# First attention: sums' inverses through memory, one value product for two query tiles, bias rows loaded four tiles ahead

## The chip, the cores and the metric

The kernel runs on one core of one Trainium2 chip. The metric is device time in microseconds (us) of one execution; the runs are of the same program, and their median is the figure.

## What is computed

The program is a transformer block with forgetting attention, then a two-layer block (RWKV, differential attention, memory attention), 1024 tokens of width 1024, all in float32. The change lies in the forgetting attention of the first block, eight heads of 64 channels:

```python
def forgetting_attention(q, k, v, log_f):
    c = jnp.cumsum(log_f, axis=1).transpose(0, 2, 1)
    ...
    scores = jnp.einsum('bqhd,bkhd->bhqk', q_i, k) * scale
    scores = scores + c_i[:, :, :, None] - c[:, :, None, :]
    scores = jnp.where(causal, scores, -jnp.inf)
    probs = jax.nn.softmax(scores, axis=-1)
    return jnp.einsum('bhqk,bkhd->bqhd', probs, v)
```

## The kernel before

`mixer` yields `att.steps_across(...)`: four pairs of heads, eight tiles of 128 queries each, 32 tiles in all. Tile iq (0 to 7) of a pair sees (iq + 1) x 128 keys. For a tile, in the names of the table `ORDER`:

- C, `Scores`: TensorE multiplies queries by keys (L1817), both heads side by side on the two halves of the array's rows, into banks 0 and 1 (head 0) and 2 and 3 (head 1). It waits for `biased` of the tile before, for those banks.
- M0 and M1, `Biased`: VectorE adds the bias of one head and takes the row maximum (L1841), then negates it (L1844). It writes one of four rows of `sc`, so it waits until the tile two before is wholly transposed. The bias comes from GpSimd, which masks a broadcast row (L2160) that SP loads once a pair (L2141).
- X0 and X1, `Exponentials`: ScalarE, with the row's sum (L1858).
- N, `Normalise`: VectorE's two reciprocals of the sums (L1867, L1869), and a wait for the second.
- V0, V1, V2, `Values`: TensorE transposes up to four 128 x 128 blocks a head (L1895) into bank 4 (head 0) and bank 5 (head 1); ScalarE copies bank 4 (L1925), VectorE bank 5 (L1934), to `pt`, four buffers of 512; TensorE multiplies by the values (L1913), the heads side by side on the halves of the array's columns. V0 transposes the first four blocks; V1 transposes the rest and multiplies the first four; V2, only for tiles 4 to 7, multiplies the rest. For tiles 0 to 3, V1 only multiplies. The product comes out transposed: channels on partitions, queries along the row.
- D, R, A, `Diagonals`, `Spread`, `ScaleAcross`: the inverses stand one to a partition but are needed along the row. ScalarE makes two diagonal matrices of them (L2101), TensorE multiplies by ones (L2114), ScalarE copies the result (L2121), and VectorE multiplies the output by it (L2129).

`ORDER` sets each engine's queue: in iteration t the engine takes each step for tile t plus the number behind the colon. Engines meet only at semaphores. TensorE does, in iteration t, V0 of t, R of t - 1, C of t + 2, V1 and V2 of t. VectorE does N and the V0 copy of t, M0 of t + 2, the V1 copy of t, M1 of t + 2, A of t - 1. Behind the last tile a `Join` stops every engine until all are done. Inside the stage two weight tiles are split by the way (L881 on GpSimd, L895 on ScalarE, L900 on VectorE).

```python
    ORDER = {
        "pe": "V0:0 R:-1 C:2 V1:0 V2:0",
        "dve": "N:0 V0:0 M0:2 V1:0 M1:2 A:-1",
        "act": "X0:1 V0:0 R:-1 D:0 V1:0 X1:1",
        "pool": "C:2",
        "sp": "C:2",
    }
```

## Time and profile before

| | us |
|---|---|
| median of three runs (lowest, highest) | 2948.1 (2946.89, 2953.39) |
| the profiled execution, its own time | 2947.62 |
| its span in the trace | 2946.4 |
| the stage: first scores of L1817 to the last L2129 | 223.6 to 365.1 |
| TensorE busy over the whole span | 2732.0 |
| mean granted TensorE clock, share of full | 0.966 |

The page gives busy time by engine, the span in slices, the chain that ended last, and the costliest groups of instructions. A float32 matmul stands as two instructions (two passes), a transpose as one. The duration of a TensorE instruction in the trace includes its way through the array, so instructions in a row overlap; what a group costs the engine is the distance from its start to the next group's start. A bracket behind a row tells the idle time ahead of it and what ended it.

### The profile page before, as it was taken

The page shows a single profiled execution, that of the slowest core. Times are in us where ns is not written, and L with a number is a line of the kernel's source. Part 1 is how long each engine was busy: PE and PEld are TensorE (multiplying, and loading weights), DVE is VectorE, ACT ScalarE, POOL GpSimd, SP SyncE. Part 2 cuts the span into 40 slices and gives each one's busy share as a digit, 9 for nine tenths or more (in the row PEclk, how much of TensorE's full clock was granted, in tenths as well). Part 3 has the DMA queues.
Part 4 walks back from the last instruction along what each step waited for, and adds up shares of the span by engine and source line. Part 5 has one row for each costly group of instructions (what it writes and reads, how often), then busy time and mean ns, then how long its engine had stood idle before and what let it go on. Part 6 is the DMA issues. An engine that isn't in the chain of part 4 may idle for free.

```text
span 2946.4 us, 49632 instructions
## 1 busy us (share of the span) xinstructions
PE 2732.0 (93%) x20750; PEld 2197.7 (75%) x20750; DVE 1372.9 (47%) x2528; ACT 926.5 (31%) x1854; POOL 634.7 (22%) x631
## 2 busy tenths in 40 slices
PE   8999989999999999999999988888879999989879
PEld 6785667888888888777888856787857878766557
DVE  4336674333333334443455306777554333366652
ACT  3226743211111111243121123444453122244441
POOL 1003253111111111325111102222113202134341
PEclk9999999999999999999999996999989999999889
DMA  3121031121111111112111210010023201122232
GB/s 122 47 72 37 22 130 58 36 72 51 43 50 51 43 50 43 51 57 86 58 32 41 75 45 2 4 32 4 4 93 114 79 15 53 39 53 55 61 81 114
DMA packets 161438, 160.33 MB, mean 54 GB/s; under 512 B 9152, under 2 KB 134714, under 8 KB 159682
## 3 DMA queue, kind: packets, MB, share of 16 engines
q1 hardware_dynamic: 161218, 157.17, 17.6%
q8 instruction: 166, 2.72, 0.4%
q14 instruction: 54, 0.44, 0.0%
HBM read 135.07 MB, written 22.08 MB: 53 GB/s over the span
## 4 chain that ended last, share of the span: by engine, by line
PE 81%; DVE 7%; ACT 4%; POOL 3%; issue 3%; DMA 3%; SPq 0%; DVEq 0%; ACTq 0%; POOLq 0%
PE ps L935 14%; PE ps L937 13%; PE ps L936 13%; PE ps L2520 7%; PE ps L990 5%; PE ps L992 5%; PE ps L991 5%; PE ps L1817 3%; PE ps L1563 2%; PE ps L1996 2%; PE ps L1565 2%; PE ps L1564 2%; DMA sb<-in_w_ffn_gate 1%; PE ps L1895 1%; DVE r L900 1%
## 5 line engine op out<-in xcount | busy, mean ns | idle before, releaser
L935 PE MATMUL ps<-r,r 128*128 128x512 f32 (+1 forms) x1760 | 698.9, 397 | 2.7 <-DVE r L900 1.9
L937 PE MATMUL ps<-r,r 128*128 128x512 f32 (+1 forms) x1760 | 684.8, 389 | 0.0
L936 PE MATMUL ps<-r,r 128*128 128x512 f32 (+1 forms) x1760 | 684.1, 389 | 0.0
L881 POOL TENSOR_TENSOR sb<-sb 128x1024 f32<-128x1024 f32 x117 | 232.2, 1994 | 1221.8 <-DMA sb<-in_w_ffn_up 482.4
L935 PEld LDWEIGHTS ps<-r,r 128*128 128x128 f32 x1760 | 332.3, 189 | 94.1 <-issue 24.2
L937 PEld LDWEIGHTS ps<-r,r 128*128 128x128 f32 x1760 | 331.9, 189 | 69.2
L936 PEld LDWEIGHTS ps<-r,r 128*128 128x128 f32 x1760 | 332.7, 189 | 66.0 <-issue 1.7
L900 DVE TENSOR_TENSOR r<-sb,r 128x1024 fp32r<-128x1024 f32 x182 | 236.6, 1317 | 306.3 <-ACT r L895 306.2
L990 PE MATMUL ps<-r,r 128*128 128x512 f32 (+1 forms) x768 | 301.9, 393 | 38.4 <-DVE r L900 16.0
L2520 PE MATMUL ps<-sb 64*64 64x64 f16 (+2 forms) x8832 | 271.0, 216 | 32.0 <-issue 11.0
L2520 PEld LDWEIGHTS ps<-sb 64*64 64x64 f32 (+1 forms) x8832 | 254.4, 126 | 56.7 <-issue 37.0
L992 PE MATMUL ps<-r,r 128*128 128x512 f32 (+1 forms) x768 | 294.1, 383 | 0.0
L991 PE MATMUL ps<-r,r 128*128 128x512 f32 (+1 forms) x768 | 293.7, 382 | 0.0
L895 ACT CAST r<-sb 128x1024 fp32r<-128x1024 f32 x182 | 186.5, 1045 | 253.1 <-POOL sb L881 203.7
L990 PEld LDWEIGHTS ps<-r,r 128*128 128x128 f32 x768 | 147.9, 193 | 74.4 <-issue 26.7
L992 PEld LDWEIGHTS ps<-r,r 128*128 128x128 f32 x768 | 147.9, 193 | 27.6
L991 PEld LDWEIGHTS ps<-r,r 128*128 128x128 f32 x768 | 148.3, 193 | 26.6 <-issue 1.2
L1563 PE MATMUL ps<-r,r 128*128 128x512 f32 x352 | 139.4, 396 | 7.6 <-DVE sb L1576 6.9
L1528 ACT CAST r<-sb 128x512 fp32r<-128x512 f32 x44 | 27.3, 621 | 378.4 <-DVE sb L1536 378.4
L1565 PE MATMUL ps<-r,r 128*128 128x512 f32 x352 | 137.6, 391 | 0.0
L1564 PE MATMUL ps<-r,r 128*128 128x512 f32 x352 | 137.6, 391 | 0.0
L1841 DVE CUSTOM_DVE_ANT_0 sb<-ps,sb 128x128 f32<-128x128 f32 (+7 forms) x160 | 120.8, 755 | 33.7 <-PE ps L1895 18.1
(266 smaller groups left out, 3421.1 us busy)
## 6 DMA issues: line engine op xcount, KB each, us to landing
sb<-in_a_w_in SPq DMA_DIRECT2D x29, 512.0 KB, 3.9
sb<-in_w_out SPq DMA_DIRECT2D x24, 512.0 KB, 5.2
sb<-in_w_ffn_gate SPq DMA_DIRECT2D x22, 512.0 KB, 4.5
sb<-in_w_ffn_up SPq DMA_DIRECT2D x22, 512.0 KB, 3.9
sb<-in_w_ffn_down SPq DMA_DIRECT2D x22, 512.0 KB, 3.5
sb<-in_w_in SPq DMA_DIRECT2D x17, 512.0 KB, 4.2
xs<-sb SPq DMA_DIRECT2D x4, 2048.0 KB, 7.1
gates<-sb SPq DMA_DIRECT2D x32, 256.0 KB, 2.1
```

Source lines behind the costliest of these rows:

```text
L881: pool.tensor_tensor(w.raw, w.raw, w.gain.unsqueeze(2).broadcast_to((P, w.nk, w.n)), ALU.mult).then_inc(*s.w_gain.up(w.id))
L900: dve.tensor_tensor(w.lo, w.raw, w.hi.bitcast(F32), ALU.subtract).then_inc(*s.w_lo.up(w.id))
L935: pe.matmul(self.out, w.hi[:, q, self.cols], hi, start=(q == 0), stop=False)
L936: pe.matmul(self.out, w.hi[:, q, self.cols], lo, start=False, stop=False)
L937: ins = pe.matmul(self.out, w.lo[:, q, self.cols], hi, start=False, stop=(q == w.nk - 1))
L990: pe.matmul(self.out, hi, w.hi[:, j, :], start=(q == 0), stop=False)
L991: pe.matmul(self.out, hi, w.lo[:, j, :], start=False, stop=False)
L992: ins = pe.matmul(self.out, lo, w.hi[:, j, :], start=False, stop=(q == nk - 1))
L1563: pe.matmul(self.out, hi, w.hi[:, 0, span_of(self.c)], start=(q == 0), stop=False)
L1564: pe.matmul(self.out, hi, w.lo[:, 0, span_of(self.c)], start=False, stop=False)
L1565: ins = pe.matmul(self.out, lo, w.hi[:, 0, span_of(self.c)], start=False, stop=(q == 1))
L2520: ins = pe.matmul(self.bank(b + p // n, n, w)[o, p % n, :], lhs[o, p], rhs[o, p], start=(j == 0 and not onto and not (keep and p)), stop=( ...
```

## The change

- `Values` is split. T0 and T1 (`TurnedAcross`) transpose blocks 0 to 3 and 4 to 7 of a tile; the copies go to `pt[h]`, one buffer a head of 8 key blocks x 2 query tiles x 128, in which an even and the next odd tile lie side by side. W (`ValuesAcross`), on odd tiles alone, multiplies both tiles at once: 256 columns for the key blocks that both see, 128 for the one that only the odd tile sees (tile 1 has three products of 128). It waits for every copy of both tiles. The copies wait until W of the tiles before has read the buffer.
- D and R on ScalarE and TensorE are gone, and with them one copy on ScalarE. N (`Inverted`) writes the reciprocals of a pair of tiles side by side and doesn't wait for itself. R (`SpreadRows`), on odd tiles, is now three DMAs on SP: the inverses to memory (2 KB in pieces of 8 bytes), and from there one row of 256 broadcast to 64 partitions for each head.
- A multiplies 256 columns at once, on odd tiles alone, two iterations behind.
- TensorE's order is T0, T1, C, W. SP takes the load of a pair's bias rows four tiles ahead in its order and, behind it, R. The load still waits until the masks of the last tile of the pair before are made.

```diff
@@ -146,7 +146,7 @@
         self.x = self.at(self.X, ST, D)
         self.ring = tuple(self.RING + j * self.SLOT for j in range(self.SLOTS))
         self.scratch = {n: nc.dram_tensor(n, shape, F32).ap() for n, shape in (
-            ("negc", [ATT_H, S]), ("xs", [P, ST, D]), ("gates", [P, KT, S]), ("memkv", [2, P, 1024]),
+            ("negc", [ATT_H, S]), ("xs", [P, ST, D]), ("gates", [P, KT, S]), ("memkv", [2, P, 1024]), ("inverse", [2 * ST, 2, P, 2]),
             ("pairs", [BT * ST // 2, P, 2]))}
         self.n_ids, self.n_banks, self.product_banks = 0, 0, 4
         self.free = {}
@@ -1653,7 +1653,7 @@
         if diff:
             self.turned = k.at(pt, ST, 2, P)
         else:
-            self.pt, self.diag = [k.at(at, HALF) for at in pt], k.at(on, 2, 2, P)
+            self.pt, self.spread = [k.at(at, ST, 2, P) for at in pt], [k.at(at, 2 * P) for at in on]
         self.heads = 1 if diff else 2
         self.per_pair = sum(self.of_tile(iq) for iq in range(ST))
 
@@ -1695,24 +1695,24 @@
         return out
 
     ORDER = {
-        "pe": "V0:0 R:-1 C:2 V1:0 V2:0",
-        "dve": "N:0 V0:0 M0:2 V1:0 M1:2 A:-1",
-        "act": "X0:1 V0:0 R:-1 D:0 V1:0 X1:1",
+        "pe": "T0:0 T1:0 C:2 W:0",
+        "dve": "N:0 T0:0 M0:2 T1:0 M1:2 A:-2",
+        "act": "X0:1 T0:0 T1:0 X1:1",
         "pool": "C:2",
-        "sp": "C:2",
+        "sp": "C:4 R:0",
     }
 
     def steps_across(self, fill=lambda t, place: []):
 
         last = self.n * ST - 1
-        kinds = {"C": (Scores,), "M0": (Biased, (0,)), "M1": (Biased, (1,)), "X0": (Exponentials, (0,)), "X1": (Exponentials, (1,)), "N": (Normalise,),
-                 "V0": (Values, 0), "V1": (Values, 1), "V2": (Values, 2), "D": (Diagonals,), "R": (Spread,), "A": (ScaleAcross,)}
+        kinds = {"C": (Scores,), "M0": (Biased, (0,)), "M1": (Biased, (1,)), "X0": (Exponentials, (0,)), "X1": (Exponentials, (1,)), "N": (Inverted,),
+                 "T0": (TurnedAcross, 0), "T1": (TurnedAcross, 1), "W": (ValuesAcross,), "R": (SpreadRows,), "A": (ScaleAcross,)}
         made, out = {}, []
-        for t in range(-3, last + 3):
+        for t in range(-4, last + 3):
             for engine, names in self.ORDER.items():
                 for name, ahead in (word.split(":") for word in names.split()):
                     at = t + int(ahead)
-                    if not 0 <= at <= last or name == "V2" and len(self.groups(*divmod(at, ST))) < 3:
+                    if not 0 <= at <= last or name == "T1" and at % ST < 4 or name in "WRA" and at % 2 == 0:
                         continue
                     if (name, at) not in made:
                         kind, *more = kinds[name]
@@ -1735,10 +1735,6 @@
 
     def of_tile(self, iq):
         return self.heads * ((self.nkeys(iq) // P + 3) // 4)
-
-    def pt_before(self, g):
-
-        return g - len(self.pt)
 
     def last_group(self, i, iq, h):
         return [g for g, h2, _, _ in self.groups(i, iq) if h2 == (0 if self.diff else h)][-1]
@@ -1877,63 +1873,6 @@
                                      ALU.mult, ALU.add).then_inc(*s.combined.up((of.id, i, iq, 0)))
 
 
-class Values(AttentionStep):
...
@@ -2089,44 +2028,118 @@
         pool.tensor_tensor(self.y, self.y, self.gate, ALU.mult).then_inc(*s.pair_gated.up((of.id, n)))
 
 
-class Diagonals(AttentionStep):
...
+class TurnedAcross(AttentionStep):
+
+    def __init__(self, k, of, i, iq, n):
+        super().__init__(k, of, i, iq)
+        self.groups = of.groups(i, iq)[2 * n:2 * n + 2]
 
     def pe(self, pe):
         k, s, of, i, iq = self.k, self.s, self.of, self.i, self.iq
+        for g, h, first, m in self.groups:
+            if first == 0:
+                pe.wait_ge(*s.exped.at((of.id, i, iq, h)))
+            k.bank_free(pe, 4 + g % 2)
+            for j in range(m):
+                ins = pe.transpose(k.ps[:, 4 + g % 2, j * P:(j + 1) * P], of.sc[:, of.buf(iq, h), (first + j) * P:(first + j + 1) * P], k.ident)
+            ins.then_inc(*s.turned_p.up((of.id, g)))
+            k.free[4 + g % 2] = (of.copied(g), (of.id, g))
+
+    def place(self, g, h, first, m):
+        return self.of.pt[h][:, first:first + m, self.iq % 2, :], self.k.ps[:, 4 + g % 2, 0:m * P].rearrange("p (a b) -> p a b", a=m)
+
+    def free(self, engine):
+        of = self.of
+        if was := of.before(self.i, self.iq, 1 + self.iq % 2):
+            engine.wait_ge(*self.s.valued.at((of.id, *was)))
+
+    def act(self, act):
+        s, of = self.s, self.of
+        for g, h, first, m in self.groups:
+            if of.copied(g) == "pt_act":
+                act.wait_ge(*s.turned_p.at((of.id, g)))
+                self.free(act)
+                act.copy(*self.place(g, h, first, m)).then_inc(*s.pt_act.up((of.id, g)))
+
+    def dve(self, dve):
+        s, of = self.s, self.of
+        for g, h, first, m in self.groups:
+            if of.copied(g) == "pt_dve":
+                dve.wait_ge(*s.turned_p.at((of.id, g)))
+                self.free(dve)
+                dve.tensor_copy(*self.place(g, h, first, m)).then_inc(*s.pt_dve.up((of.id, g)))
+
+class AcrossStep(AttentionStep):
+
+    def __init__(self, k, of, i, iq):
+        super().__init__(k, of, i, iq)
+        self.n = (i * ST + iq) // 2
+        self.bank, self.spread = 6 + self.n % 2, of.spread[self.n % 2]
+        self.inverse = k.tok[:, 3].rearrange("p a b -> p (a b)")[:, 4 * self.n:4 * self.n + 4].rearrange("p (h c) -> p h c", h=2)
+
+class Inverted(AcrossStep):
+
+    def dve(self, dve):
+        s, of, i, iq = self.s, self.of, self.i, self.iq
         for h in range(2):
+            dve.wait_ge(*s.exped.at((of.id, i, iq, h)))
+            dve.reciprocal(self.inverse[:, h, iq % 2:iq % 2 + 1], of.stat(iq, h)[:, 2:3]).then_inc(*s.inverted.up((of.id, i, iq, h)))
+
+class SpreadRows(AcrossStep):
+
+    def sp(self, sp):
+        s, of, n = self.s, self.of, self.n
+        rows = self.k.scratch["inverse"][n]
+        sp.wait_ge(*s.inverted.at((of.id, self.i, self.iq, 1)))
+        sp.dma_start(rows.rearrange("h p c -> p h c"), self.inverse).then_inc(*s.dma_inverse.up(n, 16))
+        if n > 1:
+            sp.wait_ge(*s.scaled_out.at((of.id, n - 2)))
+        sp.wait_ge(*s.dma_inverse.at(n))
+        for h in range(2):
+            sp.dma_start(self.spread[64 * h:64 * h + 64], rows[h].rearrange("p c -> (p c)").partition_broadcast(64)).then_inc(*s.dma_across.up((n, h), 16))
+
+class ValuesAcross(AcrossStep):
+
+    def pe(self, pe):
+        k, s, of, i, iq, b = self.k, self.s, self.of, self.i, self.iq, self.bank
+        k.bank_free(pe, b)
+        for g, _, first, _ in of.groups(i, iq - 1) + of.groups(i, iq):
+            pe.wait_ge(*s[of.copied(g)].at((of.id, g)))
+        heads = [(h, slice(64 * h, 64 * h + 64)) for h in range(2)]
+        both = lambda j, h, o, **at: pe.matmul(k.ps[o, b, 0:2 * P], of.v(i, j)[:, o], of.pt[h][:, j, :, :].rearrange("p a b -> p (a b)"), **at)
+        one = lambda j, c, h, o, **at: pe.matmul(k.ps[o, b, c * P:(c + 1) * P], of.v(i, j)[:, o], of.pt[h][:, j, c, :], **at)
+        if iq == 1:
+            for h, o in heads:
+                one(0, 0, h, o, start=True, stop=True)
+                one(0, 1, h, o, start=True, stop=False)
+                ins = one(1, 1, h, o, start=False, stop=True)
+        else:
+            for j in (*range(iq - 1), iq, iq - 1):
+                for h, o in heads:
+                    ins = one(j, 1, h, o, start=False, stop=False) if j == iq else both(j, h, o, start=(j == 0), stop=(j == iq - 1))
+        ins.then_inc(*s.valued.up((of.id, i, iq)))
+        k.free[b] = ("scaled_out", (of.id, self.n))
+
+class ScaleAcross(AcrossStep):
+
+    def dve(self, dve):
+        k, s, of, n, iq = self.k, self.s, self.of, self.n, self.iq
+        dve.wait_ge(*s.valued.at((of.id, self.i, iq)))
+        dve.wait_ge(*s.dma_across.at((n, 1)))
+        across = lambda a, names: a.rearrange(f"p ({names}) -> p a b", a=2)
+        dve.tensor_tensor(across(of.out(self.i)[:, (iq - 1) * P:(iq + 1) * P], "a b"), across(k.ps[:, self.bank, 0:2 * P], "a b"),
+                          across(self.spread, "b a"), ALU.mult).then_inc(*s.scaled_out.up((of.id, n)))
 
 class ForgetBiasRows:
...
@@ -3129,8 +3142,8 @@
     mix = [k.at(k.XL + (4 + j) * S, S) for j in range(4)] + mixp
     bias = ForgetBiasRows(k, F + 12288, [F + 14336, k.XH + 5632, F + 15360, k.XH + 6656])
     of_qk = lambda i: [("copied_dve" if h else "copied_act", of[5 + 4 * j + i, h].id) for j in range(2) for h in range(2)]
-    att = Attention(k, 4, lambda i: q[:, i, :], lambda i: key[:, i, :], lambda i, j: v[:, j, toks[i]], lambda i, iq: mix[i][:, toks[iq]],
-                    k.XH, (k.XH + 4096, k.XH + 4608, F + 16912, F + 17424), k.XH + 5120, lambda iq: (iq + 1) * P, bias, ready=lambda i, iq: of_v + of_qk(i))
+    att = Attention(k, 4, lambda i: q[:, i, :], lambda i: key[:, i, :], lambda i, j: v[:, j, toks[i]], lambda i: mix[i],
+                    k.XH, (k.XL, k.XL + 2048), (k.XH + 4096, k.XH + 4352), lambda iq: (iq + 1) * P, bias, ready=lambda i, iq: of_v + of_qk(i))
     mem_turned = [("turn", st.id) for st in mem]
     yield Ring(k, room + k.ring)
     yield from weave(vprods + main, *[(j + 1, [turned[j + 2], split[j + 2], *rows[j + 4:j + 5]]) for j in range(ST - 2)],
```

How the queues change. TensorE, from the scores of tile 6 (128x512 with 128x384; 128 to 128 in a transpose, 64x128 in a value or spread product) to those of tile 7, before:

```order
L1817 MATMUL ps<-sb 128x512 [waits s_biased]
L1817 MATMUL ps<-sb 128x512
L1817 MATMUL ps<-sb 128x384 x2
L1895 MATMUL ps<-sb 128x128 [waits s_pt_act]
L1895 MATMUL ps<-sb 128x128 [waits s_pt_dve]
L1913 MATMUL ps<-sb 64x128 [waits s_pt_dve,s_pt_act,s_scaled_out]
L1913 MATMUL ps<-sb 64x128 x7
L1913 MATMUL ps<-sb 64x128 [waits s_pt_dve,s_pt_act]
L1913 MATMUL ps<-sb 64x128
L1895 MATMUL ps<-sb 128x128 [waits s_pt_act,s_exped]
L1895 MATMUL ps<-sb 128x128 x3
```

Now (L1813 scores, L2045 transposes, L2118 and L2119 values), from the values of tiles 2 and 3 to the scores of tile 6, then the transposes of tile 5:

```order
L2118 MATMUL ps<-sb 64x256 x2
L2045 MATMUL ps<-sb 128x128 [waits s_pt_act,s_exped]
L2045 MATMUL ps<-sb 128x128 x3
L2045 MATMUL ps<-sb 128x128 [waits s_pt_dve,s_exped]
L2045 MATMUL ps<-sb 128x128 x3
L2045 MATMUL ps<-sb 128x128 [waits s_pt_act]
L2045 MATMUL ps<-sb 128x128 [waits s_pt_dve]
L1813 MATMUL ps<-sb 128x512 [waits s_biased]
L1813 MATMUL ps<-sb 128x512
L1813 MATMUL ps<-sb 128x384 x2
L2045 MATMUL ps<-sb 128x128 [waits s_pt_act,s_exped]
L2045 MATMUL ps<-sb 128x128 x3
```

The transposes of block 4 of tile 4 stood behind the scores of tile 6 and now stand ahead of them, right behind those of blocks 0 to 3, and the value products that followed them are gone from this place.

VectorE around the scores of tile 7, now (L2091 reciprocals, L2071 copies, L1837 bias and maximum, L2141 the scaling):

```order
L2091 RECIPROCAL sb<-sb 128x1 [waits s_exped] x2
L2071 COPY sb<-ps 128x4x128 [waits s_valued,s_turned_p]
L1837 ISA sb<-ps,sb 128x1024 [waits s_turned_p,s_bias_made,s_scored]
L1837 ISA sb 128x1
L1840 TENSOR_SCALAR sb<-sb 128x1 [waits s_biased]
L2071 COPY sb<-ps 128x2x128 [waits s_valued,s_turned_p]
L1837 ISA sb<-ps,sb 128x1024 [waits s_turned_p,s_bias_made,s_scored]
L1837 ISA sb 128x1
L1840 TENSOR_SCALAR sb<-sb 128x1 [waits s_biased]
L2141 TENSOR_TENSOR sb<-ps,sb 128x256 [waits s_dma_across,s_valued]
```

The copy of the second group (128x2x128) stands, as before, between the two heads' bias steps of the tile two ahead; the scaling comes every second tile, with 256 columns.

## Rows read from the trace of the kernel before

**Rows 1.** The page: its first line.
```profile
span 2946.4 us, 49632 instructions
```
**Rows 2.** Busy time in one period of a pair: us, PE, PEld, DVE, ACT, POOL, clock.
```profile
298.50:332.30 33.80, 32.07 (x300) 21.05 (x298) 23.37 (x85) 24.61 (x68) 10.65 (x16) 1.00 0.09 32
```
**Rows 3.** Timeline of PE, third pair: start us, us from first start to last end.
```profile
298.50 0.92 PE L1817 MATMUL ps<-sb 64*128 64x384 f32 x4
...
307.25 1.56 PE L1817 MATMUL ps<-sb 64*128 64x512 f32 x8
...
311.16 1.77 PE L1817 MATMUL ps<-sb 64*128 64x512 f32 x8
312.86 0.44 PE L1895 MATMUL ps<-sb 128*128 128x128 f32 x2
...
315.02 0.44 PE L1913 MATMUL ps<-sb 128*64 128x128 f32 x4 [0.69 <-DVE sb L1934]
315.39 1.09 PE L1895 MATMUL ps<-sb 128*128 128x128 f32 x8
316.41 0.44 PE L2114 MATMUL ps<-sb 128*64 128x128 f32 x4
316.78 1.99 PE L1817 MATMUL ps<-sb 64*128 64x512 f32 x8
...
321.23 0.66 PE L1913 MATMUL ps<-sb 128*64 128x128 f32 x8 [0.85 <-DVE sb L1934]
...
323.21 0.49 PE L1817 MATMUL ps<-sb 64*128 64x128 f32 x4
...
327.67 0.70 PE L1817 MATMUL ps<-sb 64*128 64x256 f32 x4
...
332.28 0.92 PE L1817 MATMUL ps<-sb 64*128 64x384 f32 x4
```
**Rows 4.** Timeline of DVE, same stretch.
```profile
313.37 1.09 DVE L1841 CUSTOM_DVE_ANT_0 sb<-ps,sb 128x896 f32<-128x896 f32 x1 [1.17 <-PE ps L1895]
...
314.58 0.29 DVE L1934 COPY sb<-ps 128x128 f32<-128x128 f32 x1
...
319.31 1.23 DVE L1841 CUSTOM_DVE_ANT_0 sb<-ps,sb 128x1024 f32<-128x1024 f32 x1 [2.05 <-PE ps L1895]
...
320.66 0.42 DVE L1934 COPY sb<-ps 128x256 f32<-128x256 f32 x1
...
324.36 0.29 DVE L1841 CUSTOM_DVE_ANT_0 sb<-ps,sb 128x128 f32<-128x128 f32 x1 [0.66 <-PE ps L1895]
...
324.77 0.56 DVE L1934 COPY sb<-ps 128x384 f32<-128x384 f32 x1
...
329.13 0.42 DVE L1841 CUSTOM_DVE_ANT_0 sb<-ps,sb 128x256 f32<-128x256 f32 x1 [0.98 <-PE ps L1895]
...
329.68 0.69 DVE L1934 COPY sb<-ps 128x512 f32<-128x512 f32 x1
```
**Rows 5.** Groups by line in the stage: busy us, mean ns, then idle before.
```profile
L2101 ACT ACTIVATE sb<-sb 128x128 f32<-128x128 f32 x64 | 22.2, 398 | 1.0 <-DVE sb L1869 1.0
```
**Rows 6.** The page's DMA issues: count, KB each, median us to landing.
```profile
sb<-pairs SPq DMA_DIRECT2D x24, 128.0 KB, 4.2
...
pairs<-sb SPq DMA_DIRECT2D x24, 1.0 KB, 3.0
```
**Rows 7.** Timeline at the stage's end: last scores, last scaling.
```profile
350.55 1.99 PE L1817 MATMUL ps<-sb 64*128 64x512 f32 x8
...
364.79 0.29 DVE L2129 TENSOR_TENSOR sb<-ps,sb 128x128 f32<-128x128 f32 x1 [1.60 <-ACT sb L2121]
```
**Rows 8.** Busy time of stretches with little TensorE work; columns as in rows 2.
```profile
222.00:226.00 4.00, 2.12 (x12) 1.05 (x11) 1.73 (x8) 0.95 (x4) 1.72 (x4) 0.93 0.40 131
226.00:230.00 4.00, 3.49 (x14) 1.63 (x13) 2.68 (x14) 2.45 (x9) 1.91 (x3) 0.50 0.00 0
2770.00:2774.00 4.00, 1.81 (x12) 0.83 (x8) 2.76 (x8) 2.20 (x7) 1.66 (x3) 1.00 0.48 164
```

71 lines of the change are left out of this document (removed).

## The prediction

> **What bounds the kernel now.** I read the page first [rows 1]: 2946.4 us, TensorE busy nearly throughout. The change touches one stage of some 140 us, so I went on to the busy times of one pair of heads in it [rows 2]: in 33.8 us TensorE is busy 32.07, VectorE 23.37, ScalarE 24.61, at full clock. ScalarE has 9 us to spare, so what the change takes from it, two 128x128 activations a tile of 398 ns [rows 5] and a copy, is worth nothing by itself. Then the timeline, from scores to scores (C of a tile; the starts are in rows 3). It shows which step ends last at each place, and where TensorE does wait: 0.69 us for VectorE's copy of tile 4's fifth block, 0.85 for the copy at tile 5 [rows 3]. Otherwise one TensorE group follows another, so before, the queue order covers nearly every copy. Two latencies are read off: VectorE's copy ends at 314.87 (314.58 + 0.29) and TensorE goes on at 315.02, 0.15 later [rows 3, 4]; from TensorE's end to the other engine I take 0.05.
>
> **TensorE's work.** A group costs the distance to the next start. Eight transposes with the spread behind them take 1.39 (315.39 to 316.78), of which the spread is 0.37; the eight take 1.02, two of them 0.37 by their shape (0.44 against 1.09) [rows 3]. Scores cost 0.213 more for each 128 keys (0.49 for 128, 1.99 for 1024), for both heads together. A value group of four instructions, one block, is 0.44 and one of eight, two blocks, 0.66 [rows 3]: 0.22 a block, again for both heads together, so the heads already run side by side at the rate of the columns. 256 columns in one instruction keep the column count: 36 blocks a pair before and after, at 0.213 each with 0.16 at the head of a group. W of tiles 1, 3, 5, 7 has 3, 7, 11, 15 blocks: 0.80, 1.65, 2.50, 3.36, sum 8.3. Before, the same columns stood in 12 groups: 36 x 0.213 + 12 x 0.16 = 9.6. So a pair saves 1.3 there, 8 x 0.37 = 3.0 for the spreads and 4 x 0.16 = 0.6 where T1 now follows T0: 4.9 us of TensorE work a pair, 20 in all. That is the gain if TensorE stays the bound.
>
> **The order around it.** It doesn't stay the bound, by my walk through one pair. VectorE's occupancy, start to start: one bias step of 896 keys 1.21, of 1024 keys 1.35; a copy of 1, 2, 3, 4 blocks ends 0.29, 0.42, 0.56, 0.69 after its start [rows 4]. Four intervals get other terms:
>
> - Scores 5 to 6 (3.91 before, from 307.25 to 311.16). TensorE now does the scores 1.49, W of tiles 2 and 3 1.65, four blocks a head of tile 4 with their way through the array 1.09. T1 needs the same banks, so it waits for VectorE's copy: 0.05 + 0.69 + 0.15, and only then a last transpose, 0.15 with its turn, and the scores. Sum 5.3: **+1.4**. Before, the scores ran beside that copy.
> - Scores 6 to 7 (5.62). Scores 1.77, 0.05, bias step 1.21, copy 0.29, 0.15: at 3.5 head 1 of tile 5 gets bank 5; transposes 0.66; VectorE is meanwhile in the second bias step and its reciprocals until 4.6; copy 0.69, 0.15, two more transposes 0.25. Sum 5.7: **+0.1**.
> - Scores 7 to 0 (6.43). W of tiles 4 and 5 waits for the copy of tile 5's blocks 4 and 5, which stands behind the bias step of tile 7: 1.99 + 0.05 + 1.35 + 0.42 + 0.15 = 3.95. W 2.50, transposes of tile 6 1.09, then again copy 0.05 + 0.69 + 0.15 and three transposes 0.35: 8.8, **+2.4**.
> - Scores 0 to 1 (4.46). No value products now; the banks cost a bias step 0.41, a copy 0.56, transposes, a copy, transposes: 3.7, **-0.8**.
> - Scores 1 to 2 (4.61). 0.70, bias step 0.55, copy 0.69, latencies 0.2: W of tiles 6 and 7 starts at 2.1, takes 3.36, then two transposes 0.37: 5.9, **+1.3**.
>
> Scores 2 to 5 took 8.75 (298.50 to 307.25) and are bound by the loop scores, bias of both heads, scores, which stays: -0.1 for the spread gone at its head. Sum **+4.2 a pair**: 38.0 for 33.8. TensorE would be busy 32.07 - 4.9 = 27 of 38.
>
> **DMAs and the end.** The inverses' way is a write and two reads. The second attention does the like: 3.0 us to landing for the write, 4.2 for a read of 128 KB [rows 6], so some 7.5 here (bounds 6 and 10, for pieces of 8 bytes and two heads). A stands two iterations behind, over 8 us later everywhere, so it is hidden inside the stage; SP has no other load queued there but the bias rows, once a pair, whose condition (masks of the last tile made) is met before it comes up, and which land two tiles early. The page *DMA: Bandwidth & Descriptors* of the Trainium skill (Latency and other measured facts) has a fixed cost of about 2.0 us for a transfer; by that the way would be some 4 us, and the end below 3 shorter. At the end nothing covers it. Before, the last scores of 1024 keys start at 350.55 and the last scaling ends at 365.08, 14.5 later [rows 7]. Now, counted from those scores: tile 6 transposed and copied at 9.6, tile 7's reciprocals at 10.3, its copies done at 13.3, W at 16.7; the inverses land at 10.3 + 0.1 + 7.5 = 17.9, the scaling ends at 18.4: **+3.9**, and +1.4 in the fourth pair's scores 5 to 6 ahead of it, less 0.1.
>
> Sum: three pairs at 4.2, less some 0.6 because a weight tile's split in the second pair (1.6 us on VectorE) costs less where TensorE waits anyway, plus 5.2: **17 us**, 0.6%. Against the profiled execution's own 2947.62 that is 2965; the median of the runs, 2948.1, lies 0.5 above it. I forecast **2966**.
>
> **Rivals.**
> *The clock falls too.* In 222 to 226 TensorE was busy 2.12 of 4 us; then its granted clock was 0.50, that is 1.2 GHz, through 226 to 230. But at 2770 to 2774 it was busy 1.81 of 4 and kept 2.4 GHz [rows 8]. Between scores 6 and 7 there are now 4 us in which it does only some 1.3 of transposes, and 2 us of nothing ahead of W of tiles 4 and 5. Each fall puts some 3 us of work at half speed: scores of tile 7 1.9 more, part of W. Once a pair that is 12 us more: 2978; twice in some pairs 2985. The page *TensorE: Matmul & The Clock Gate* (Part 4: PE-mode transpose) says transposes don't count as work for the clock as matmuls do; by that rule the fall comes in every pair, 2978 or over. Rows 8 can't tell it, so I keep it a rival.
> *TensorE stays the bound.* If the copies came early enough, because queues overlap more than my walk allows, 20 us of work go and the end gives back 4: 2932, faster. It decides where T1 of tile 4 starts: right behind T0, and the 1.2 us of copy and turns between aren't there. Against it: banks 4 and 5 are single, and rows 3 show TensorE already waiting on just such copies.
> *They cancel.* The waits are half of what I walked, 2.1 of the 4.2 and more overlapped: within 6 us of 2948. Speaks for it that each interval adds small terms; against it that the same terms give the 5.62 and 6.43 of before within 0.1.
> *The way through memory is slow,* over 12 us: A then holds VectorE's queue, and the reciprocals, copies and bias steps behind it: 2 us for each pair of tiles, 16 times, 2998. The rows of the second attention speak against it.
>
> **How the numbers follow.** A change of 0.2%, 6 us, is about what a measurement can tell. Forecast (2956 to 2975): 0.58. Clock: 0.20. TensorE the bound: 0.11. They cancel: 0.08. Slow memory: 0.03. So faster 0.11, same 0.08, slower 0.81. The range leaves out the gain and the slow way, and most of cancelling: 2954 to 2987.
>
> **What would show it.** Scores of tile 2 to scores of tile 2 a pair later: 38, not 33.8 (under 33: I am wrong). Idle ahead of T1 of tile 4 on VectorE's copy; W of tiles 5 and 7 waiting 2.0 and 1.4 us on VectorE's copy. VectorE idle at the last scaling on the DMA, some 1.5. Scaling elsewhere without a wait. The granted clock of the stage 1.00 behind its first 10 us; if it is under 0.95, the clock rival holds.

## The result, and the profile after

| | before | after |
|---|---|---|
| median of the runs, us (lowest, highest; four runs each) | 2950.74 (2946.89, 2955.24) | 2971.79 (2969.46, 2980.59) |
| the profiled execution, its own time | 2947.62 | 2969.49 |
| its span | 2946.4 | 2968.2 |
| the stage, first scores to the end of the last scaling | 223.63 to 365.08: 141.45 | 222.83 to 381.96: 159.13 |
| last scores of 1024 keys to the end of the last scaling | 14.5 | 19.7 |
| one pair of heads, scores of tile 2 to scores of tile 2, third to fourth | 33.78 | 37.98 |

The ratio is 1.0079, with an interval of 1.0063 to 1.0095: the change is slower, by 21 us of 2951. The forecast was 2966, with 2954 to 2987 around it.

The busy time of the pair of heads that answers to [rows 2], in the columns of [rows 2]. TensorE has 2.8 us less to do and the pair takes 4.2 us more; the clock is full.

```profile
304.59:342.57 37.98, 29.31 (x205) 17.94 (x204) 22.77 (x80) 18.13 (x44) 10.61 (x16) 1.00 0.21 42
```

The timeline of TensorE in that pair, which answers to [rows 3]: start, us to the last end, line, and in the bracket the idle time ahead of it. In the changed kernel L1813 is the scores, L2045 the transposes, L2118 and L2119 the joint values.

```profile
304.59 0.92 PE L1813 MATMUL ps<-sb 64*128 64x384 f32 x4
...
313.31 1.56 PE L1813 MATMUL ps<-sb 64*128 64x512 f32 x8 [1.00 <-DVE sb L1837]
...
317.80 0.33 PE L2045 MATMUL ps<-sb 128*128 128x128 f32 x1 [0.24 <-ACT sb L2063]
318.34 0.33 PE L2045 MATMUL ps<-sb 128*128 128x128 f32 x1 [0.21 <-DVE sb L2071]
318.60 1.77 PE L1813 MATMUL ps<-sb 64*128 64x512 f32 x8
320.30 0.66 PE L2045 MATMUL ps<-sb 128*128 128x128 f32 x4
322.05 0.63 PE L2045 MATMUL ps<-sb 128*128 128x128 f32 x4 [1.09 <-DVE sb L2071]
323.38 0.93 PE L2045 MATMUL ps<-sb 128*128 128x128 f32 x4 [0.70 <-ACT sb L2063]
324.24 1.99 PE L1813 MATMUL ps<-sb 64*128 64x512 f32 x8
328.18 1.95 PE L2118 MATMUL ps<-sb 128*64 128x256 f32 x16 [1.95 <-DVE sb L2071]
...
333.06 0.49 PE L1813 MATMUL ps<-sb 64*128 64x128 f32 x4
...
336.70 0.70 PE L1813 MATMUL ps<-sb 64*128 64x256 f32 x4
338.81 2.81 PE L2118 MATMUL ps<-sb 128*64 128x256 f32 x24 [1.42 <-DVE sb L2071]
...
342.57 0.92 PE L1813 MATMUL ps<-sb 64*128 64x384 f32 x4
```

Behind the scores of tile 7 (324.24) TensorE is done at 326.2 and stands for 1.95 us. What it waits for is seen on VectorE, whose timeline of the same stretch is next (it answers to [rows 4]): the bias step of head 0 starts when the scores are there, at 326.26, and the 0.42 us copy of tile 5's last two blocks stands behind it and ends at 328.03. The joint values start 0.15 later, at 328.18.

```profile
326.26 1.23 DVE L1837 CUSTOM_DVE_ANT_0 sb<-ps,sb 128x1024 f32<-128x1024 f32 x1 [2.44 <-PE ps L1813]
...
327.61 0.42 DVE L2071 COPY sb<-ps 128x256 f32<-128x256 f32 x1
328.13 1.23 DVE L1837 CUSTOM_DVE_ANT_0 sb<-ps,sb 128x1024 f32<-128x1024 f32 x1
```

The waits of the whole stage, of TensorE and one of VectorE: who waited for whom, us in total, times, longest. The last of these rows is the only wait of VectorE on the way through memory.

```profile
PE ps L2118 <- DVE sb L2071: 12.9, 8, 1.9
...
PE ps L1813 <- DVE sb L1837: 9.4, 10, 1.1
...
PE ps L2045 <- DVE sb L2071: 7.0, 13, 1.1
...
PE ps L2045 <- ACT sb L2063: 4.7, 12, 0.7
DVE sb L2141 <- DMA sb<-inverse: 4.5, 1, 4.5
```

The end of the stage, where that wait stands: SP's timeline with the write of the inverses and their two reads, and VectorE's with the last scaling. From the issue of the write to the scaling it is 7.46 us.

```profile
374.08 0.37 SPq L2101 DMA_DIRECT2D inverse<-sb  x1
378.20 1.08 SPq L2106 DMA_DIRECT2D sb<-inverse  x2
```

```profile
381.54 0.42 DVE L2141 TENSOR_TENSOR sb<-ps,sb 128x256 f32<-128x256 f32 x1 [4.48 <-DMA sb<-inverse]
```

The page's DMA issues of the new transfers, with the columns of [rows 6]:

```profile
sb<-inverse SPq DMA_DIRECT2D x32, 64.0 KB, 2.8
...
inverse<-sb SPq DMA_DIRECT2D x16, 2.0 KB, 3.3
```

### The profile page after: what moved, and what is told of

It reads as the page before. It is cut to its first block, busy times and chain, and to the rows that moved or that the text cites. A ratio compares the mean times of both kernels' runs of the same rounds, so it can differ in the third digit from the quotient of the medians.

```text
span 2968.2 us, 48830 instructions
## 1 busy us (share of the span) xinstructions
PE 2723.2 (92%) x20382; PEld 2186.4 (74%) x20382; DVE 1370.3 (46%) x2512; ACT 900.0 (30%) x1758; POOL 634.2 (21%) x631
## 4 chain that ended last, share of the span: by engine, by line
PE 79%; DVE 8%; ACT 4%; POOL 3%; issue 3%; DMA 3%; SPq 0%; DVEq 0%; ACTq 0%; POOLq 0%
PE ps L935 13%; PE ps L937 13%; PE ps L936 13%; PE ps L2533 7%; PE ps L990 5%; PE ps L992 5%; PE ps L991 5%; PE ps L1813 3%; PE ps L1563 2%; PE ps L1935 2%; PE ps L1565 2%; PE ps L1564 2%; DMA sb<-in_w_ffn_gate 1%; DVE sb L1837 1%; DVE r L900 1%
## 5 line engine op out<-in xcount | busy, mean ns | idle before, releaser
L990 PE MATMUL ps<-r,r 128*128 128x512 f32 (+1 forms) x768 | 302.0, 393 | 41.1 <-DVE r L900 16.7
L1563 PE MATMUL ps<-r,r 128*128 128x512 f32 x352 | 139.2, 395 | 7.3 <-DVE sb L1576 6.6
L1854 ACT ACTIVATE sb<-sb 128x128 f32<-128x128 f32 (+7 forms) x160 | 123.3, 773 | 67.1 <-DVE sb L1840 67.1
L1837 DVE CUSTOM_DVE_ANT_0 sb<-ps,sb 128x128 f32<-128x128 f32 (+7 forms) x160 | 120.7, 755 | 40.8 <-PE ps L1813 40.7
L1565 PE MATMUL ps<-r,r 128*128 128x512 f32 x352 | 137.6, 391 | 0.0
```

Source lines behind the costliest of these rows:

```text
L990: pe.matmul(self.out, hi, w.hi[:, j, :], start=(q == 0), stop=False)
L1563: pe.matmul(self.out, hi, w.hi[:, 0, span_of(self.c)], start=(q == 0), stop=False)
L1565: ins = pe.matmul(self.out, lo, w.hi[:, 0, span_of(self.c)], start=False, stop=(q == 1))
```

## Experiments

Each kernel was run beside the kernel before, whose median was 2947.97 to 2950.31 in these sets. "Period" is the distance from the scores of tile 2 in the third pair of heads to those in the fourth; "end" is from the start of the last scores of 1024 keys to the end of the last scaling.

| kernel | inverses | values | period | end | median | ratio, interval |
|---|---|---|---|---|---|---|
| before | ones | by tile | 33.78 | 14.5 | 2950.74 | |
| the change | memory | joint | 37.98 | 19.7 | 2971.79 | 1.0079, 1.0063 to 1.0095 |
| scores ahead of second transposes | memory | joint | 35.64 | 18.1 | 2963.64 | 1.0049, 1.0032 to 1.0065 |
| VectorE's second copy early | memory | joint | 34.29 | 16.0 | 2957.78 | 1.0025, 1.0012 to 1.0037 |
| memory alone | memory | by tile | 32.08 | 16.2 | 2941.88 | 0.9977, 0.9966 to 0.9987 |
| joint values alone | ones | joint | 40.81 | 19.7 | 2972.20 | 1.0075, 1.0058 to 1.0093 |
| woven orders | memory | joint | 38.36 | 18.0 | 2974.84 | 1.0086, 1.0073 to 1.0099 |
| memory alone, copy early | memory | by tile | 31.43 | 15.9 | 2939.44 | 0.9969, 0.9958 to 0.9981 |
| loads ahead alone | ones | by tile | 33.77 | 14.5 | 2950.58 | 1.0008, 0.9998 to 1.0018 |
| before, copy early | ones | by tile | 32.37 | 14.4 | 2944.98 | 0.9982, 0.9972 to 0.9991 |
| divided wait | memory | joint | 32.72 | 16.6 | 2950.77 | 1.0005, 0.9994 to 1.0016 |
| divided wait, copy early | memory | joint | 34.19 | 18.0 | 2947.31 | 0.9994, 0.9981 to 1.0007 |
| way made longer | memory | by tile | 43.70 | 20.4 | 2966.39 | 1.0065, 1.0048 to 1.0082 |
| memory alone, copy early, end by ones | memory | by tile | 31.42 | 14.7 | 2939.29 | 0.9971, 0.9960 to 0.9982 |

### Order alone: the scores ahead of the second transposes

```diff
-        "pe": "T0:0 T1:0 C:2 W:0",
+        "pe": "T0:0 C:2 T1:0 W:0",
```

> The change with one word of TensorE's order moved: the scores of two tiles ahead stand ahead of the second half of a tile's transposes, where the change has them behind it. THEORY A, the order of the queues: in the change the scores of tiles 5 and 7 begin only after both halves of the transposes, and wait in them for the copies that free the two banks. Walked through with the durations of the change's profile, a steady pair of heads falls from 38.0 to 36.5 us (scores of tile 2 to scores of tile 2), the wait of the values of tiles 5 and 7 on VectorE's copy stays near 2 us, and the time is some 6 us below the change's, 2963 to 2966. THEORY B, the work itself (slower 256-wide products, the way through memory, the pieces of the copies): the order changes nothing, the period stays within 0.3 of 38.0 and the time within 2 us of the change's. THEORY C, that bias steps set the pace of both: the scores come out earlier but VectorE adds the bias no sooner, so the wait moves from the values to the scores, and the time is the change's or up to 4 us above it.

Measured: 35.64 a pair, 8 us below the change. Theory A, and by more than walked (36.5). The scores now run beside the first copies. What is left is the wait of the joint values, which A had put near 2 us; TensorE's timeline shows 1.88 and 1.12 in the steady pair:

```profile
324.14 1.95 PE L2118 MATMUL ps<-sb 128*64 128x256 f32 x16 [1.88 <-DVE sb L2071]
...
333.80 2.81 PE L2118 MATMUL ps<-sb 128*64 128x256 f32 x24 [1.12 <-DVE sb L2071]
```

### Order alone: VectorE's second copy early

```diff
-        "dve": "N:0 T0:0 M0:2 T1:0 M1:2 A:-2",
+        "dve": "N:0 T0:0 T1:0 M0:2 M1:2 A:-2",
```

> The change with one word of VectorE's order moved: its copy of the second half of a tile's transposes stands ahead of the first bias step of two tiles on, where the change has it behind it. THEORY A, the order of the queues: the 1.95 and 1.42 us that the values of tiles 5 and 7 wait on VectorE's copy in the change's profile go away, since the copy no longer stands behind a bias step of about 1.2 us that itself waits for scores queued behind those transposes. The walk gives 34.5 us for a steady pair instead of 38.0, and a time some 14 us below the change's, 2955 to 2959: still above the kernel before, by the longer end of the stage and some 0.7 us a pair. THEORY B, the work itself: the wait goes from the values to the scores' buffers, the period stays over 37.5 and the time within 3 us of the change's. THEORY C, the later bias step now delays the exponentials: the period rises above 38.0 and the time is 2 to 8 us above the change's.

Measured: 34.29 a pair (walked: 34.5) and 14 us below the change, theory A. One word of VectorE's queue is worth two thirds of what the change lost. The waits of the values shrink from 12.9 us to 1.6; what remains is the first copy, seen by the transposes (10.5 us on ScalarE's, in which the exponential stands ahead):

```profile
PE ps L2045 <- ACT sb L2063: 10.5, 15, 2.0
...
PE ps L2118 <- DVE sb L2071: 1.6, 4, 0.9
```

### The parts apart: memory alone, and joint values alone

The first takes over `Values` of the kernel before, with four buffers; products of tile iq go to columns iq % 2 of a shared bank, so that L2137 scales two tiles.

```diff
-        "pe": "T0:0 T1:0 C:2 W:0",
-        "dve": "N:0 T0:0 M0:2 T1:0 M1:2 A:-2",
-        "act": "X0:1 T0:0 T1:0 X1:1",
+        "pe": "V0:0 C:2 V1:0 V2:0",
+        "dve": "N:0 V0:0 M0:2 V1:0 M1:2 A:-2",
+        "act": "X0:1 V0:0 V1:0 X1:1",
```

> One part of the change alone: the inverse sums are spread through memory and one 256-wide scaling by VectorE takes two tiles, but the values are multiplied tile by tile, from four buffers and in the order of the kernel before. Nothing else is left of the old spreading (no diagonals, no products with ones, no copy by ScalarE). THEORY A, the loss of the change belongs to the joint values: this kernel's steady pair comes to 31 to 32 us (33.8 before, 38.0 in the change), as TensorE loses the products with ones and ScalarE three small operations a tile. The end of the stage is some 4 us longer than before's 14.5, by the way through memory of about 7.5 us in the change's profile. The time is 2940 to 2945, below the kernel before. THEORY B, the loss belongs to the way through memory (its two transfers in a row, or the load of the bias rows queued behind them): the period is 36 or more and the time 2960 or more. THEORY C, the old spreading was hidden anyway: the period is 33.5 to 34, and the time the kernel before's plus the longer end, 2952 to 2956.

The second keeps the change's order and buffers, and spreads by ones:

```diff
-        "pe": "T0:0 T1:0 C:2 W:0",
-        "act": "X0:1 T0:0 T1:0 X1:1",
-        "sp": "C:4 R:0",
+        "pe": "T0:0 R:-1 T1:0 C:2 W:0",
+        "act": "X0:1 T0:0 T1:0 X1:1 R:-1 D:0",
+        "sp": "C:4",
```

> The other part of the change alone: the values of two tiles are multiplied together as in the change, in its order of the queues and with its two buffers, but the inverse sums are spread as in the kernel before, by ScalarE's diagonals, TensorE's products with ones and a copy. THEORY A, the loss belongs to the joint values: the steady pair stays at 38 to 39.5 us and waits in the same places; only the end of the stage is some 4 us shorter, since no transfer stands there. The time is 2966 to 2976. THEORY B, the loss belongs to the way through memory: the period is 34 to 35.5 and the time 2950 to 2958. THEORY C, the two add up through the same queue: the small operations on TensorE and ScalarE now lie in the exposed part, the period is over 40 and the time over 2978.

Measured: 32.08 and 2941.9, theory A: memory alone is faster than the kernel before; its end, 16.2, is 1.7 us longer and not 4. Joint values alone give 40.81 a pair at 2972.2: the time is A's, the period as it stands C's. But some 1.6 of the 40.81 is a fall of the clock, once in each steady pair of this execution; without it 39.2 are left, which is A's. This is TensorE's timeline there, and the granted clock was 0.64 in 334 to 338 (the columns of [rows 2]). In the change the same sixteen instructions took 1.95, in its row at 328.18 above.

```profile
334.93 3.54 PE L2140 MATMUL ps<-sb 128*64 128x256 f32 x16 [1.95 <-DVE sb L2072]
```

```profile
334.00:338.00 4.00, 3.07 (x16) 2.25 (x18) 2.62 (x10) 1.24 (x2) 0.80 (x2) 0.64 0.01 2
```

A missed the end of this kernel: it was to be some 4 us shorter than the change's, and is 19.7 like the change's, with a fall of the clock in both. No transfer stands there, but TensorE does the last product with ones only behind the last joint values, and the last scaling waits for ScalarE's copy of it:

```profile
391.08 0.42 DVE L2162 TENSOR_TENSOR sb<-ps,sb 128x256 f32<-128x256 f32 x1 [4.00 <-ACT sb L2129]
```

So the four kernels make a square. Joint values cost 7.0 a pair with ones (33.78 to 40.81; 5.4 without the fall of the clock) and 5.9 with memory (32.08 to 37.98). Memory gains 1.7 with values by tile and 2.8 with joint ones (1.2 without the fall). The loss is the joint values' in this order. The way through memory is a gain inside the stage, and at its end a loss of 1.7 with values by tile (14.5 to 16.2) and none with joint ones.

### The third part alone: loads ahead

```diff
-        "sp": "C:2",
+        "sp": "C:4",
```

> The kernel before with the third part of the change alone: SP's loads of the bias rows four tiles ahead instead of two. In the trace of the kernel before no operation of VectorE or GpSimd waits for these rows in a steady pair. THEORY A: nothing follows, the period is 33.8 and the time within 2 us of the kernel before, 2948 to 2952. THEORY B, an earlier load collides with another transfer or waits for its buffer in SP's queue, ahead of loads of weights: 2 to 4 us slower.

Measured: 33.77 a pair, 2950.6. Nothing follows from it, as A said.

### Woven orders

```diff
-        "dve": "N:0 T0:0 M0:2 T1:0 M1:2 A:-2",
-        "act": "X0:1 T0:0 T1:0 X1:1",
+        "dve": "N:0 T1:0 M0:2 T0:1 M1:2 A:-2",
+        "act": "T0:0 X0:1 T1:0 X1:1",
```

> The whole change, with other orders on VectorE and ScalarE. On VectorE the copy of the second half of the transposes stands first, and the copy of the next tile's first half between the two bias steps; on ScalarE the copy of the first half stands ahead of the exponential. In the run with VectorE's second copy moved ahead, the two waits that are left are TensorE's on the copies of the first half, 1.99 us in tile 5, behind two bias steps and an exponential. THEORY A, the order of the queues is all that is wrong with the joint values: both waits shrink, and a steady pair comes to 32.5 to 33.5 us (38.0 in the change, 34.3 with the one copy moved), the time to 2949 to 2954. THEORY B, the joint values cost something of their own that no order takes away, because nothing of a tile's values can run while its halves are copied: the period stays at 34 to 35 and the time at 2955 to 2960.

Measured: 38.36 and 2974.8, outside both theories. The copy of the next tile's first half waits for transposes that TensorE does only behind the joint values; the second bias step stands behind that copy, and the scores wait for it. In TensorE's timeline the scores' waits are:

```profile
313.62 1.13 PE L1813 MATMUL ps<-sb 64*128 64x512 f32 x4 [1.14 <-DVE sb L1837]
...
317.98 1.35 PE L1813 MATMUL ps<-sb 64*128 64x512 f32 x8 [1.35 <-DVE sb L1837]
...
321.97 1.56 PE L1813 MATMUL ps<-sb 64*128 64x512 f32 x8 [1.61 <-DVE sb L1837]
```

I had looked only at the copies whose wait I wanted gone, and not at what was queued behind them.

### Is it the joint values, or that their first product waits for everything?

On top of the order with the scores ahead, the joint values wait for the copies of the second halves only where they use them:

```diff
-        for g, _, first, _ in of.groups(i, iq - 1) + of.groups(i, iq):
-            pe.wait_ge(*s[of.copied(g)].at((of.id, g)))
+        copied = lambda groups: [pe.wait_ge(*s[of.copied(g)].at((of.id, g))) for g, _, _, _ in groups]
+        late = [group for group in of.groups(i, iq) if group[2]]
+        copied(of.groups(i, iq - 1) + of.groups(i, iq)[:2])
...
             for j in (*range(iq - 1), iq, iq - 1):
+                if j == 4 and iq > 5 or j == iq == 5:
+                    copied(late)
```

> The whole change with its joint values, the scores ahead of the second half of the transposes, and the wait of the joint values divided: the products of the first four blocks of keys wait for the copies of the first halves alone, and only those behind them for the copies of the second halves. The run with the scores ahead alone stands at 35.6 us a pair, of which its values wait 11.7 us in eight places on VectorE's copy, 2.9 a pair. THEORY A, the joint values as such cost nothing, and what costs is that their first product waits for all halves of two tiles: some 1 to 2 us of products cover the second copies, the 2.9 go, and the period comes to 32.3 to 33.3 us, the time to 2945 to 2951. THEORY B, the joint values cost by their size or by coming once in two tiles: the wait only moves to the scores, which wait for bias steps: the period stays over 34.5 and the time over 2955.

Measured: 32.72 a pair and 2950.8, theory A. The values start right behind the transposes, without a wait, where they had waited 1.88:

```profile
317.07 0.66 PE L2045 MATMUL ps<-sb 128*128 128x128 f32 x4
317.66 1.95 PE L2119 MATMUL ps<-sb 128*64 128x256 f32 x16
```

So 5.3 of the 5.9 us that joint values cost in this pair belong to the order and to the one wait, and not to products over two tiles. The rest (32.72 against 32.08) I didn't take apart. The median follows only in part: 2950.8 is 21 us below the change, and is still the kernel before's and 9 us over memory alone. In the trace the stage is 141.6 us long, as long as before (141.45) and 5.2 longer than with memory alone: the end is 16.6 where before had 14.5, and the clock fell in the second pair (0.59 in 272 to 276).

> The run with the divided wait, and on top VectorE's second copy ahead of the first bias step, as in the two runs where that gave 3.7 and 1.4 us a pair. THEORY A, the order of VectorE's copy and the order of TensorE's scores help each other: 31.5 to 32.3 us a pair. THEORY B, with the scores ahead of the second transposes the copy waits longer than the bias step would, as in the run with the woven orders, where the bias steps stood behind a copy that came late and the scores waited 0.7 to 1.9 us in nearly every tile: the period is 33 to 35 us, above that of the run with the divided wait alone, and the time 2950 to 2960. I take B.

This one adds VectorE's early copy to it. Measured: 34.19, with a fall of the clock in it: the scores of tile 7 in the third pair took 3.49 instead of 1.99. From the scores of tile 7 to those of tile 0 it is 7.70 here and 6.06 in the second pair, where the clock didn't fall; with that the period is 32.55. Neither theory: the copy early gives nothing here (its wait, 0.93 ahead of the scores of tile 7, has taken the place of 0.38), and it doesn't cost what B said. The times, 2950.8 and 2947.3, don't tell the two apart.

```profile
313.76 3.49 PE L1813 MATMUL ps<-sb 64*128 64x512 f32 x8 [0.93 <-DVE sb L1837]
```

### The copy early, with values by tile

Both kernels with values by tile get the same one-word move:

```diff
-        "dve": "N:0 V0:0 M0:2 V1:0 M1:2 A:-2",
+        "dve": "N:0 V0:0 V1:0 M0:2 M1:2 A:-2",
```

> The inverse sums through memory and values tile by tile, with VectorE's second copy ahead of the first bias step. In the run without that move, the values of tiles 5 and 7 (second product group) waited 0.69 and 0.85 us on that copy, and the scores 0.2 to 0.5 us on the second bias step in four tiles. THEORY A: both waits on the copy vanish, the bias steps come up to 0.4 us later, and a steady pair falls from 32.1 to 30.8 to 31.5 us; the time is 3 to 5 us below that run, 2937 to 2939. THEORY B, the later bias step is passed on to the scores in every tile: the period stays at 32 to 32.5 and the time at 2941 to 2944.

> The kernel before with VectorE's second copy ahead of the first bias step, and nothing else. In its trace the second group of values waits 0.69 us in tile 5 and 0.85 us in tile 7 on that copy. THEORY A, the mechanism that costs the change 3.7 us a pair is there in the kernel before too, only smaller: the period falls from 33.8 to 32.5 to 33.2 and the time by 2 to 5 us, to 2945 to 2948. THEORY B, TensorE's products with ones cover whatever the move gives: the period stays within 0.3 of 33.8 and the time within 1.5 us.

Measured: 31.43 and 2939.4 with memory, 32.37 and 2945.0 in the kernel before, theory A twice; the first median lies 0.4 above the range given, and the second period 0.1 below its range. The two waits that the expectations name, 0.69 and 0.85, stand at the values of tiles 4 and 5 [rows 3], not 5 and 7. They were there before the change. In the change TensorE waits 1.09 for the same copy of tile 4 (322.05, ahead of transposes) and 1.95 for that of tile 5; the 1.42 at tile 7 is new, where the values of before had no wait.

### How much cover the way through memory has

```diff
-        sp.dma_start(rows.rearrange("h p c -> p h c"), self.inverse).then_inc(*s.dma_inverse.up(n, 16))
+        sp.dma_start(rows.rearrange("h p c -> p h c"), self.inverse).then_inc(*s.dma_inverse_once.up(n, 16))
+        sp.wait_ge(*s.dma_inverse_once.at(n))
+        sp.dma_start(rows.rearrange("h p c -> p h c"), self.inverse).then_inc(*s.dma_inverse.up(n, 16))
```

> The run with the memory alone (values tile by tile), where the sums are written twice, one write behind the other, before they are read: the way through memory grows by one write, 3.3 us, from 7.5 to some 10.8. In that run the shortest cover of the way in a steady pair is 10.0 us, from the reciprocals of tile 1 (296.1) to the scaling (306.1). THEORY A, the way is hidden by its cover: a steady pair grows by 0 to 0.8 us from 32.1, and only the end grows by some 3.3; the time is 3 to 6 us above that run's 2941.9. THEORY B, the writes and reads also hold up SP's queue (the loads of bias rows and of weights behind them): the period grows by 2 us or more and the time by 10 or more.

Measured: 43.70 a pair and 24.5 us more than without the second write: theory B, and more than it said. SP's timeline shows why. SP waits for each write before it issues what follows, so the ways of two pairs of tiles can't overlap: the reads of one stand 10.4, 8.4, 14.4 and 8.4 us behind those of the one before (the next two are at 336.34 and 344.75), 41.6 together, and the load of the bias rows comes in between. In the run with one write the reads of the third pair stand 7.3, 6.5, 8.5 and 9.0 us apart, so a turn of 8.4 no longer fits the two shorter ones. VectorE then waits ten times in the stage for the inverses, 23.0 us, 6.7 of them at the end.

```profile
303.11 1.09 SPq L2128 DMA_DIRECT2D sb<-inverse  x2
304.24 0.59 SPq L2121 DMA_DIRECT2D inverse<-sb  x1
309.60 0.36 SPq L2123 DMA_DIRECT2D inverse<-sb  x1
313.53 1.09 SPq L2128 DMA_DIRECT2D sb<-inverse  x2
314.67 0.59 SPq L2121 DMA_DIRECT2D inverse<-sb  x1
318.12 0.36 SPq L2123 DMA_DIRECT2D inverse<-sb  x1
321.96 2.88 SPq L2128 DMA_DIRECT2D sb<-inverse  x2
```

With one write SP has by my estimate a turn of about 5 us for each way (3.3 for the write to land, 1.1 for the issue of the reads, 0.4 for that of the write, from the rows of the change), 20 of the 32 us of a pair.

### The end by ones

The fastest kernel, with the last two tiles of the stage spread by diagonals, ones and a copy (classes as in the kernel before):

```diff
+ or name == "R" and at == last or name in "DO" and at < last - 1
...
-        dve.wait_ge(*s.dma_across.at((n, 1)))
+        by_ones = n == of.n * ST // 2 - 1
+        dve.wait_ge(*(s.spread_copied.at((of.id, n)) if by_ones else s.dma_across.at((n, 1))))
```

> The fastest run so far (inverse sums through memory, values tile by tile, VectorE's second copy early), with the last two tiles of the stage spread by diagonals, products with ones and a copy instead of through memory. In that run's trace the last scaling waits 2.85 us for its transfer and the stage ends 15.9 us after the start of the last scores; in the run of the kernel before with the copy early it is 14.4. THEORY A, the end is longer by the way through memory alone: the wait on the transfer goes, some 1 us of products with ones and copy comes in its place, the end falls to 14 to 14.5 and the steady pair stays at 31.4; the time is 1 to 3 us below that run's 2939.4. THEORY B, the end is bound by the values, and the ones delay them by as much as the transfer did: the end stays at 15.5 to 16 and the time within 1 us.

Measured: the end is 14.7 (15.9 without) and the period 31.42, theory A as far as the trace goes, though the end lies 0.2 above A's range: the last scaling waits 1.64 for the copy instead of 2.85 for the transfer. The median, 2939.3, shows nothing of the 1.2 us, which is what B said of the time. This is smaller than a measurement can tell.

```profile
353.68 0.42 DVE L2169 TENSOR_TENSOR sb<-ps,sb 128x256 f32<-128x256 f32 x1 [1.64 <-ACT sb L2142]
```

## Why the prediction was right, and where it wasn't

The forecast was slower, 2966, by one walk through a pair; measured are 2971.8. Its steps against the trace after, in us from scores to scores:

| scores | forecast | measured |
|---|---|---|
| 2 to 5 | 8.65 | 8.72 |
| 5 to 6 | 5.3 | 5.29 |
| 6 to 7 | 5.7 | 5.64 |
| 7 to 0 | 8.8 | 8.82 |
| 0 to 1 | 3.7 | 3.64 |
| 1 to 2 | 5.9 | 5.87 |
| the pair | 38.0 | 37.98 |

**The period** is right to 0.1 in every interval, and so are the waits it named: 1.95 and 1.42 ahead of the joint values for 2.0 and 1.4, and idle time ahead of the second transposes of tile 4. The runs show that it was right for its reason: moving the copy from behind the bias step gave back 3.7 a pair, moving the scores 2.3, and dividing the wait on top 2.9.

**TensorE's work** was forecast to fall by 4.9 a pair, to 27. The busy time fell by 2.8, to 29.31 [rows 2], and the pair's 37.98 less the eleven idle times in TensorE's brackets (8.6) gives the same 29.4: the term was 2.1 too large. The joint values explain little of it: from their start to the next group's they cost 8.65 in that pair, for 8.3 forecast. I didn't take the rest apart. The walk didn't use this sum, so the period came out without it; a forecast with TensorE as the bound would have been off by it.

**The way through memory** took 7.46 us at the end for 7.5 forecast, and its scalings wait nowhere else. The Trainium skill's page *DMA: Bandwidth & Descriptors* (Latency and other measured facts) has some 2.0 us of fixed cost a transfer, from which the forecast estimated a way of 4 us; the landing times of this case, 3.3 for the write in pieces of 8 bytes and 2.8 for a read, are over it, and the way is nearly twice as long. "Hidden inside the stage" was right, but its reason was incomplete: it looked at the distance in time and not at how long SP itself is held. The run with the longer way shows that SP's turn is what limits it.

**The end** was forecast 3.9 longer, and is 5.2 longer (19.7 for 14.5). Counted from the last scores (362.23), TensorE's joint values end at 18.1 for 16.7 forecast, and the scaling starts at 19.3 for 17.9 forecast: the transfer ends 1.2 behind the values, as walked. (The bracket's 4.48 counts from where VectorE had nothing else to do. The forecast's sign, VectorE idle for some 1.5, was wrong as written; the part of the wait that is the transfer's alone is the 1.2.) Both come 1.4 late because the clock had fallen, to 0.64 of full in 366 to 370, a fall that the forecast held for a rival: the joint values of tiles 4 and 5 held TensorE for 4.0 us instead of 2.5, and tile 7's reciprocals, behind them, are ready at 11.8 instead of 10.3. So of the 5.2, some 1.4 is the clock's, 1.2 the transfer's, and the rest the joint values' own longer end; joint values alone, with no transfer there, ended as late (19.7). These are TensorE's last rows of the stage:

```profile
376.88 2.81 PE L2118 MATMUL ps<-sb 128*64 128x256 f32 x24 [0.88 <-DVE sb L2071]
379.49 0.42 PE L2119 MATMUL ps<-sb 128*64 128x128 f32 x4
379.71 0.63 PE L2118 MATMUL ps<-sb 128*64 128x256 f32 x4
```

**The clock** was 1.00 in the pair read above, but not in every pair: it fell in the second pair and at the end. This is the row of the second pair, in which sixteen instructions of the joint values took 3.6 us instead of 1.95; ahead of it TensorE had been busy 1.99 of 3.93 us.

```profile
284.57:288.50 3.93, 1.99 (x9) 0.71 (x9) 1.88 (x5) 1.48 (x3) 0.64 (x2) 1.00 0.05 4
288.50:292.50 4.00, 4.00 (x24) 2.81 (x24) 1.63 (x6) 0.78 (x2) 0.40 (x1) 0.57 0.13 33
```

So the stage's mean was 0.98, above the 0.95 below which the clock rival was to hold. Yet each fall cost 1.4 to 1.7 us (scores 7 to 0 took 10.50 in the second pair for 8.82), about half of the 3 that the rival gave it, and "1.00 behind the first 10 us" was wrong. On the other side, the fall that stood at the start of the stage before [rows 8] isn't there in this execution of the change. Eleven of the fourteen kernels have it in their trace and three don't, one of them the kernel before with the copy early, so its absence is not the change's doing. By the Trainium skill's page *TensorE: Matmul & The Clock Gate* (Part 4: PE-mode transpose) transposes don't count as busy for the clock as matmuls do, and the forecast took from it a fall in every pair. The trace of the change doesn't bear that out: the same stretch between the scores of 6 and 7 stands in all four pairs, and two of them had no fall. The run with joint values alone had one in each pair. Which of the two it will be can't be said from these rows.

**The sum.** The stage is 17.7 us longer; 17 was forecast for it, and three of its terms were off by more than 1 us and cancel. The period was read rightly; that the stage's sum came out within 1 us is luck. The first pair took 2.0 more (37.96 for 35.96, and not 4.2, as the fall of the clock in [rows 8] stayed out), the second 5.0 (40.53 for 35.54: 4.2, less 0.9 for the weight split, where 0.6 was forecast, and 1.7 for the clock), the third 4.2, the fourth to its last scores 1.4 and the end 5.2, less 0.1 at the start. In the profiled executions, what is missing of the measured 21 lies in later code that the change doesn't touch. From the last weights of L1563 (at 1252.1 before and 1267.8 after, so already 15.7 behind) to the end, the same 14801 TensorE instructions took 1694.3 us before and 1700.4 after:

```profile
1252.10:2946.40 1694.30, 1537.27 (x14801) 1237.79 (x14799) 830.00 (x1647) 567.00 (x1211) 403.37 (x396) 0.95 0.18 52
```

```profile
1267.80:2968.20 1700.40, 1540.97 (x14801) 1239.49 (x14799) 830.96 (x1647) 566.70 (x1211) 403.96 (x396) 0.95 0.18 52
```

Over the fourteen kernels of this study this stretch took 1689.6 to 1703.0 us in the profiled execution, and not in the order of their stages (1693.8 with joint values alone, 1703.0 with the end by ones). So joint values alone, 9 us behind the change at that place, ends 2.5 us behind it in its profiled execution. This spread needn't belong to the kernels: in one set the kernel before alone took 2943.9 to 2957.6 us over 23 executions, 13.7 us, and the profiled execution with the end by ones was the slowest of its nine (2945.0, lowest 2936.2). I didn't find what sets it, and with one trace of each kernel the two can't be told apart. The 5 us between the forecast and the median are within that spread.

**The rivals.** "TensorE stays the bound" was wrong: banks 4 and 5 are single and the copies were as exposed as walked. "They cancel" as well. "Slow memory" is excluded by the 7.46 us of the way and by the memory-alone run, which is faster than the kernel before.

## What to carry to other kernels

A step that collects several products into one also collects their waits: the first product now waits for the last operand. Before joining, look at which copies the separate steps ran beside; if the joined step is kept, let each product wait for its own operand only, or put its last copy ahead of any long operation that itself waits (on top of the divided wait, the early copy gave nothing here). A transfer for whose landing a queue waits is not hidden by distance alone: add up how long each turn holds that queue, and compare it with the period and with the distance between two turns. And undo the parts of a change one by one: here one part gained 8 us (2950 to 2942) and was buried under another that cost 30 (2942 to 2972).
